# Attention of a transformer layer: values held in TensorE, probabilities streamed, output left turned

## The chip, the cores and the metric

The kernel runs on one core of a Trainium2 chip. The metric is the device time of one execution in microseconds (us). Matrix products run on TensorE (PE in the profile; its weight loads are shown as PEld), elementwise work on VectorE (DVE), ScalarE (ACT) and GpSimd (POOL), and SyncE (SP) issues nearly all weight transfers.

## The reference, cut to what matters

One layer on 256 tokens of width 2048: feed-forward, attention mixer, feed-forward, gated embedding. Everything is float32. The change lies in the mixer:

```
z = rmsnorm(h, g_mix_pre) @ w_qkv + b_qkv          # 2048 x 4352
oa = dilated_attention(qa, ka, va)                  # 16 heads of 64; three patterns, (128,1) (512,4) (2048,16)
ob = sink_swa_gqa(qb, kb, vb, sinks)                # 16 query heads, 2 key/value heads, window 127, sinks
o = concat(rmsnorm(oa, g_out_a), rmsnorm(ob, g_out_b)) @ w_o + b_o
h = h + rmsnorm(o, g_mix_post)
```

With 256 tokens the three dilated patterns share keys: a key that n patterns see counts n times in numerator and divisor, so head a computes softmax(score + log n) over the 256 keys. Queries of the first 128 tokens see 128 keys, those of the second 128 see all 256: three blocks of 128 x 128 for each head. The sinks add one exponential to each divisor of ob.

## The kernel before, in words

TensorE does one long stream of slots. A slot is a chunk of 256 rows x 512 columns of a weight matrix: SP loads it to `raw` (ring of 4), ACT rounds it to `w_high` (L888), DVE subtracts to get `w_rest` (L1201), and TensorE makes 12 matmuls of 512 columns (3 products x 2 row chunks x 2 token tiles; `products`, L470 to L472). A slot's buffer is free once TensorE has used the slot (`w_used`), and `w_rest_done` lets TensorE in. So ACT and DVE work up to four slots ahead.

In the mixer the slots are counted by L: 68 slots of w_qkv (nine blocks of columns, the order is QKV_BLOCKS), then 32 of w_o. Each engine runs its own loop over L, written out in Python, and the small work of attention is hung on fixed values of L, after the slot's matmuls on TensorE. This fixes the order on every engine; only semaphores tie the engines together.

Heads go in 16 pairs of two, the eight pairs of ob first. For each pair, every four slots:

- `turn_pair` (L703): transposes of q (and k), 2 or 4 of 128 x 128, into `pair_bank`; ACT copies (`pair_out`), DVE takes the rest (`pair_rest`, L1470).
- `scores` (L730): 18 products, the two heads on the two halves of the array's rows (64 rows each), L748.
- DVE `soften` (L1440): adds distance times slope to the scores (L1445), two maxima, negated peak. ACT `exps` (L1058): exponentials into `prob`.
- `turn_prob` (L755): three transposes of 128 x 128 for each head, L758. ACT (ob) copies them to `prob_T` or DVE (oa) multiplies them by the turned counts (`prob_T_out`, L1475).
- `weigh` (L762): for each head three float32 products, with a block of `prob_T` stationary (128 x 128) and the values moving (66 columns: 64 and two of ones, whose sum is the divisor), L771 to L773, to `o_bank`.
- DVE `pair_o` (L1482): reciprocal of the divisor, times `o_bank`, into `z`.

The counts are turned once (`turn_count`, three transposes). Then `turn_o` (L780) transposes o back in eight units of four transposes (L569 with `z`), ACT and DVE make `x_high` and `x_rest` from them, and the slots of w_o use these. ACT squares o for the two norms (`square_o`), POOL makes the factors (`factor`, L426). Before the change POOL does nothing else in the mixer than such factors on single columns.

Of the kernel before, what the change touches and what calls it, by code (L numbers as in the profile page):

```python
# [9 lines left out]

# [13 lines left out]
P = 128  # L24
NB = 512
# [9 lines left out]
VW = HD + 2  # L35


def layer_program(nc, x, p, g_ffn1_pre, w_ffn1_gate, w_ffn1_up, w_ffn1_down, g_ffn1_post,
# [60 lines left out]
    U_O = U_MIX + XU  # L99
    U_X2 = U_O + XU  # L100
# [11 lines left out]
    OBLK = AW // NB  # L112
# [11 lines left out]
    def norm_width(job):  # L124
        return AW if job in (J_OA, J_OB) else D

    squares = [T * (OBLK if j in (J_OA, J_OB) else NBD) for j in range(NJOB)]
# [8 lines left out]
    HALVES = [(0, 0), (1, 0), (0, 1), (1, 1)] + [(nb, half) for nb in range(2, NBD) for half in range(2)]  # L136
    WO_SLOTS = ([(hb, k) for hb in (0, 1) for k in range(HU)] + [(hb, k) for hb in (2, 3) for k in range(HU, XU - 1)]
                + [(hb, XU - 1) for hb in (2, 3)]
                + [(hb, HU * HALVES[hb][1] + k) for hb in range(4, 2 * NBD) for k in range(HU)])
# [12 lines left out]
    L_HEAD = L_KEYS + 1  # L152
    L_PAIR = [L_KEYS - 1] + [L_HEAD + 4 * pr - 2 for pr in range(1, PAIRS - 2)] + [L_HEAD + 4 * PAIRS - 11, L_HEAD + 4 * PAIRS - 5]
    L_COUNT = L_PAIR[5] + 2

    G_VALS = BH + AH // 2
    WEIGH_AT = [L_HEAD + 2 * h + 2 for h in range(G_VALS)] + [NSLOT + d for d in (0, 1, 3, 3, 5, 6, 8, 10)]
    PAIR_O_AT = [L_HEAD + 4 * q + 5 for q in range(G_VALS // 2)] + [NSLOT + d for d in (2, 4, 7, 11)]

    O_TURN_AT = [NSLOT - KS + 1 + k for k in range(HU)] + [NSLOT + d for d in (2, 4, 7, 12)]  # L160
    assert len(WEIGH_AT) == H and len(PAIR_O_AT) == PAIRS and len(O_TURN_AT) == XU
# [18 lines left out]
    with ExitStack() as ctx:  # L180
# [48 lines left out]
        vals = sb("vals", [P, T, AH + KVH, VW])  # L229
        bias_row = sb("bias_row", [P, QKV])  # L230
        k_swap = sb("k_swap", [P, T, KVH * HD])
        kb_high = sb("kb_high", [P, 2, S], F32R)
        kb_rest = sb("kb_rest", [P, 2, S], F32R)
        qk_high = sb("qk_high", [P, 2, 2, S], F32R)
        qk_rest = sb("qk_rest", [P, 2, 2, S], F32R)
        dist_i = sb("dist_i", [P, 3 * P], I32)
# [5 lines left out]
        count_T = sb("count_T", [P, 3 * P])  # L242
# [3 lines left out]
        prob_T = sb("prob_T", [P, PTR, 3 * P])  # L246
        peak = sb("peak", [P, 2, T])
# [63 lines left out]
        def wait_prob_T(eng, h):  # L311

            if h < BH:
                eng.wait_ge(prob_T_b, h + 1)
            else:
                eng.wait_ge(prob_T_a, h - BH + 1)
# [1345 lines left out]
```

## Time and profile before

| | |
|---|---|
| median of 3 runs (range) | 1927.27 us (1927.13 to 1927.98) |
| the profiled execution | 1927.2 us |
| its span | 1925.3 us |
| busy: PE, PEld, DVE, ACT, POOL | 1911.9, 1586.7, 1046.8, 875.5, 45.2 us |
| granted TensorE clock | 0.999 |

The span is the time between the first and the last instruction of the profile; the execution has 1.9 us more around it. Busy is the sum of an engine's instruction times. Matmuls overlap, so a matmul's own duration (390 ns for 512 columns) is not what it costs: that is the distance from its start to the start of the next.

### The profile page before, as it was taken

What the parts mean: (1) busy time and instruction counts of PE and PEld (TensorE: products, weight loads), DVE (VectorE), ACT (ScalarE), POOL (GpSimd) and SP (SyncE); (2) the same over time, 40 slices, a digit from 0 to 9 for tenths busy, and PEclk for the clock granted to TensorE, in tenths of its full rate; (3) what the DMA queues carried; (4) which work ended last, traced back from release to release, by engine and by line L of the source; (5) the groups of instructions that cost most, each with busy time, mean ns of one, the idle gap of its engine ahead of it and who ended that gap; (6) DMA issues with size and microseconds to landing.
All of it is one profiled execution on the core that took longest, in us unless ns stands there. A gap on an engine that the chain in (4) does not pass through costs nothing.

```text
span 1925.3 us, 24947 instructions
## 1 busy us (share of the span) xinstructions
PE 1911.9 (99%) x8929; PEld 1586.7 (82%) x8929; DVE 1046.8 (54%) x1199; ACT 875.5 (45%) x1125; POOL 45.2 (2%) x102
## 2 busy tenths in 40 slices
PE   9999999999999999999999999999999999999998
PEld 8888888888888888888888788888888888888886
DVE  5445445444544447676776754454554554444575
ACT  6444444444344346445455644444444444344563
POOL 1000000000000001000000100000000000000010
PEclk9999999999999999999999999999999999999999
DMA  7666666666565655655455466666666666656554
GB/s 249 189 187 192 187 189 186 190 187 191 194 200 194 202 196 163 194 153 165 151 176 181 149 206 191 191 188 193 187 189 191 185 192 201 202 192 203 193 189 142
DMA packets 188484, 361.06 MB, mean 188 GB/s; under 512 B 11440, under 2 KB 16000, under 8 KB 188032
## 3 DMA queue, kind: packets, MB, share of 16 engines
q1 hardware_dynamic: 187408, 356.69, 61.0%
q10 hardware_dynamic: 1008, 3.46, 0.5%
q8 instruction: 43, 0.70, 0.1%
q14 instruction: 25, 0.20, 0.0%
HBM read 358.01 MB, written 2.10 MB: 187 GB/s over the span
## 4 chain that ended last, share of the span: by engine, by line
PE 98%; DVE 1%; ACT 0%; issue 0%; POOL 0%; DVEq 0%; POOLq 0%; ACTq 0%
PE bank L470 31%; PE bank L472 31%; PE bank L471 31%; PE bank L569 2%; PE bank L748 1%; PE bank L758 1%; DVE w_rest L1201 0%; PE bank L772 0%; PE bank L773 0%; PE bank L610 0%; PE bank L771 0%; DVE resid L1225 0%; PE bank L716 0%; DVE x_rest L1216 0%; ACT w_high L888 0%
## 5 line engine op out<-in xcount | busy, mean ns | idle before, releaser
L1201 DVE TENSOR_TENSOR w_rest<-raw,w_high 128x1024 fp32r<-128x1024 f32 x656 | 802.0, 1224 | 757.8 <-ACT w_high L888 757.0
L888 ACT CAST w_high<-raw 128x1024 fp32r<-128x1024 f32 x656 | 686.9, 1049 | 901.9 <-PE bank L472 900.3
L470 PE MATMUL bank<-w_high,x_high 128*128 128x512 f32 (+1 forms) x1920 | 754.3, 393 | 0.5 <-issue 0.2
L472 PE MATMUL bank<-w_high,x_rest 128*128 128x512 f32 (+1 forms) x1920 | 745.1, 388 | 0.0
L471 PE MATMUL bank<-w_rest,x_high 128*128 128x512 f32 (+1 forms) x1920 | 743.9, 387 | 0.0
L472 PEld LDWEIGHTS bank<-w_high,x_rest 128*128 128x128 f32 x1920 | 360.5, 188 | 74.9
L470 PEld LDWEIGHTS bank<-w_high,x_high 128*128 128x128 f32 x1920 | 360.7, 188 | 73.8 <-issue 2.6
L471 PEld LDWEIGHTS bank<-w_rest,x_high 128*128 128x128 f32 x1920 | 361.0, 188 | 70.5
L470 PE MATMUL bank<-w_high,h_high 128*128 128x512 f32 x704 | 274.2, 390 | 0.0
L472 PE MATMUL bank<-w_high,h_rest 128*128 128x512 f32 x704 | 273.9, 389 | 0.0
L471 PE MATMUL bank<-w_rest,h_high 128*128 128x512 f32 x704 | 273.9, 389 | 0.0
L471 PEld LDWEIGHTS bank<-w_rest,h_high 128*128 128x128 f32 x704 | 132.2, 188 | 27.5
L470 PEld LDWEIGHTS bank<-w_high,h_high 128*128 128x128 f32 x704 | 132.2, 188 | 27.5
L472 PEld LDWEIGHTS bank<-w_high,h_rest 128*128 128x128 f32 x704 | 132.2, 188 | 27.0
L431 POOL TENSOR_SCALAR msq<-stat 128x1 f32<-128x1 f32 x20 | 6.2, 308 | 1619.8 <-ACT junk L899 1619.2
L962 ACT ACTIVATE branch<-bank,rstd 128x512 f32<-128x512 f32 x44 | 27.9, 686 | 34.7 <-PE bank L472 32.4
L1216 DVE SCALAR_TENSOR_TENSOR x_rest<-bank,gain_T,x_high 128x256 fp32r<-128x256 f32 x68 | 29.7, 478 | 22.7 <-ACT x_high L913 22.5
L913 ACT ACTIVATE x_high<-bank,gain_T 128x256 fp32r<-128x256 f32 x68 | 28.5, 471 | 20.9 <-PE bank L569 18.1
L1312 DVE SCALAR_TENSOR_TENSOR branch<-bank,rstd,branch 128x512 f32<-128x512 f32 x44 | 31.0, 747 | 9.8 <-PE bank L472 9.8
L1062 ACT ACTIVATE prob<-score,neg_peak 128x256 f32<-128x256 f32 x32 | 16.3, 510 | 32.6 <-DVE neg_peak L1457 16.5
L435 POOL TENSOR_TENSOR msq<-msq,stat 128x1 f32<-128x1 f32 x52 | 24.6, 474 | 240.2 <-ACT junk L899 237.3
L1322 DVE TENSOR_TENSOR h_rest<-bank,h_high 128x512 f32 (+1 forms) x44 | 28.2, 683 | 2.3 <-ACT h_high L970 2.3
(147 smaller groups left out, 675.2 us busy)
## 6 DMA issues: line engine op xcount, KB each, us to landing
raw<-in_w_ffn_gate SPq DMA_DIRECT2D x176, 512.0 KB, 4.4
raw<-in_w_ffn_up SPq DMA_DIRECT2D x176, 512.0 KB, 3.7
raw<-in_w_ffn_down SPq DMA_DIRECT2D x176, 512.0 KB, 4.1
raw<-in_w_qkv SPq DMA_DIRECT2D x68, 512.0 KB, 3.8
raw<-in_w_o SPq DMA_DIRECT2D x32, 512.0 KB, 3.7
raw<-in_w_ple_gate SPq DMA_DIRECT2D x32, 512.0 KB, 4.4
resid<-in_x SPq DMA_DIRECT2D x8, 256.0 KB, 6.7
gain_row<-in_g_ffn_post SPq DMA_DIRECT2D x8, 256.0 KB, 3.8
```

The source lines that it names most:

```text
L435: step(nc.gpsimd.tensor_tensor(msq[:, job, t:t + 1], msq[:, job, t:t + 1], part[b], ALU.add))
L470: nc.tensor.matmul(o[:, 0:width], xh, wh, start=first and c == 0, stop=False)
L471: nc.tensor.matmul(o[:, 0:width], xh, wr, start=False, stop=False)
L472: ins = nc.tensor.matmul(o[:, 0:width], xr, wh, start=False, stop=last and c == chunks - 1)
L569: ins = nc.tensor.transpose(b[:, (c * T + t) * P:(c * T + t + 1) * P], src(t, c), ident[:])
L888: nc.scalar.copy(slot(n, k)[0], raw[:, k]).then_inc(w_high_done, 1)
L913: ins = nc.scalar.activation(x_high[:, CPS * k + c, :], b[:, c * S:(c + 1) * S], ACT.Copy, scale=gain_T[:, gain + c:gain + c + 1])
L962: ins = nc.scalar.activation(silu_g[:, t, :], acc[b0 % 2][t][:], ACT.Silu, scale=rstd[:, job, t:t + 1])
L1201: nc.vector.tensor_tensor(to_rest, raw[:, k], to_high.bitcast(F32), ALU.subtract).then_inc(w_rest_done, 1)
L1216: ins = nc.vector.scalar_tensor_tensor(out=x_rest[:, CPS * k + c, :], in0=b[:, c * S:(c + 1) * S], scalar=gain_T[:, gain + c:gain + c + 1] ...
L1312: ins = nc.vector.scalar_tensor_tensor(out=hidden[:, t, :], in0=acc[(b0 + 1) % 2][t][:], scalar=rstd[:, job, t:t + 1], in1=silu_g[:, t, :] ...
L1322: nc.vector.tensor_tensor(h_rest[:, chunks, :], turn[j][:].rearrange("p (c s) -> p c s", c=CPS), h_high[:, chunks, :].bitcast(F32), ALU.su ...
```

## The change

- `weigh` works on a pair: the values of a head (128 x 64) are stationary, `prob_T` moves. The keys of the first tile go over all 256 queries, those of the second over 128 queries ("two pieces"). The output of the even head goes to partitions 0 to 63 of `o_bank`, that of the odd head to 64 to 127, and it is o transposed. Four products a pair in place of six. `turn_prob` puts its blocks in another order for this and does both heads of a pair behind one another.
- There are no columns of ones in `vals`. The exponentials' instructions on ACT give their sums (`accum_out`), DVE adds the sink and takes the reciprocal (`normalise`), and POOL multiplies `prob` by it (`scale_probs`) before `turn_prob`.
- As o comes out turned, `turn_o` is gone. ACT copies `o_bank` to `z` (`o_out`) and makes `x_high` from it (`o_unit`), DVE makes `x_rest` (`o_rest_unit`).
- The log of the counts is added to the scores instead of multiplying the probabilities: `turn_count` and DVE's `prob_T_out` are gone, POOL prepares a table for each head of oa (`table_of`) and `soften` adds it. ACT copies `prob_T` of all 32 heads (`prob_out`).
- The squares for the norms are made by POOL (`square_pair`) and summed over partitions by TensorE (`sum_squares`, two products with two columns, twice), and DVE copies the sums (`sums_out`).
- The heads start four slots later (L_HEAD = 18 for 14) and the last weighing is at slot 14 of w_o. The slots of w_o go through all four column blocks of the first half of rows and then of the second.
- `bias_row` holds 2048 columns as a ring of four blocks; `gain_mix` has a place of its own and is loaded behind the last scores.

```diff
-    HALVES = [(0, 0), (1, 0), (0, 1), (1, 1)] + [(nb, half) for nb in range(2, NBD) for half in range(2)]
+    HALVES = [(nb, half) for half in range(2) for nb in range(NBD)]
+    WO_SLOTS = [(hb, HU * HALVES[hb][1] + k) for hb in range(2 * NBD) for k in range(HU)]
...
-    L_HEAD = L_KEYS + 1
+    L_HEAD = L_KEYS + 5
+    L_SCORE = [L_HEAD + 4 * p for p in range(PAIRS)]
+    L_PAIR = [L_KEYS - 1] + L_SCORE[:-1]
+    L_PROB = [at + 3 for at in L_SCORE]
+    L_WEIGH = [at + 4 for at in L_SCORE]
+    L_SUM = [L_PROB[PAIRS_B + 1], L_WEIGH[-1] + 2]
+    O_AT = [NSLOT - KS + 1 + k for k in range(HU)] + [NSLOT - 2, NSLOT, L_WEIGH[13] + 1, L_WEIGH[15] + 1]
...
+            def scale_probs(g):
+                pool.wait_ge(norm_ready, g + 1)
+                step(nc.gpsimd.tensor_scalar(prob[:, g % 2, 0:S], prob[:, g % 2, 0:S], norm[:, g % 2, 1:2], None,
+                                             ALU.mult))
+                nc.gpsimd.tensor_scalar(prob[:, g % 2, S:S + P], prob[:, g % 2, S:S + P], norm[:, g % 2, 0:1], None,
+                                        ALU.mult).then_inc(prob_ready, 1)
+            def square_pair(q):
+                pool.wait_ge(o_ready, q + 1)
+                half, o = q // PAIRS_B, o_place(q)
+                to = square_tmp[:] if q % PAIRS_B else o_square[:, half, :]
+                ins = nc.gpsimd.tensor_tensor(to.rearrange("p (t n) -> p t n", t=T), o, o, ALU.mult)
+                step(ins)
+                if q % PAIRS_B:
+                    step(nc.gpsimd.tensor_tensor(o_square[:, half, :], o_square[:, half, :], square_tmp[:], ALU.add))
...
+            def table_of(g):
+                if g - 2 >= BH:
+                    pool.wait_ge(scores_read, g - 1)
+                step(nc.gpsimd.tensor_scalar(tab[:, g % 2, :], dist_a[:], -head_slope[g] * HD ** 0.5, None, ALU.mult))
+                nc.gpsimd.tensor_tensor(tab[:, g % 2, :], tab[:, g % 2, :], count[:], ALU.add).then_inc(tab_ready, 1)
+            for pr in range(PAIRS):
+                scale_probs(2 * pr)
+                scale_probs(2 * pr + 1)
+                if pr:
+                    square_pair(pr - 1)
+                if pr == PAIRS_B - 1:
+                    pool.wait_ge(tables_ready, 1)
+                if PAIRS_B - 1 <= pr < PAIRS - 1:
+                    table_of(2 * pr + 2)
+                    table_of(2 * pr + 3)
...
-            def weigh(h):
-                wait_prob_T(pe, h)
...
-                nc.tensor.matmul(o[1], w[:, 0:P], vals[:, 0, v, :], start=True, stop=False)
-                nc.tensor.matmul(o[1], w[:, P:2 * P], vals[:, 1, v, :], start=False, stop=True)
-                nc.tensor.matmul(o[0], w[:, 2 * P:3 * P], vals[:, 0, v, :], start=True, stop=True
-                                 ).then_inc(weighed, 1)
+            def weigh(q):
+                pe.wait_ge(prob_T_ready, 2 * q + 2)
+                pe.wait_ge(z_ready, 2 if q < PAIRS_B else 6 if q < PAIRS_B + PAIRS_B // 2 else 9)
+                if q:
+                    pe.wait_ge(o_ready, q)
+                if q == PAIRS_B + 1:
+                    pe.wait_ge(o_summed, 1)
+                for c, keys, queries in ((0, slice(0, S), slice(0, S)), (1, slice(S, S + P), slice(P, S))):
+                    for h in range(2):
+                        g = 2 * q + h
+                        v = AH + g // (BH // KVH) if g < BH else g - BH
+                        ins = nc.tensor.matmul(o_bank[HD * h:HD * h + HD, queries], vals[:, c, v, :],
+                                               prob_T[:, g % PTR, keys], start=c == 0, stop=c == 1)
+                ins.then_inc(weighed, 1)
+            def sum_squares(half):
+                pe.wait_ge(part_ready, 1)
+                pe.wait_ge(o_squared, half + 1)
+                pe.wait_ge(o_ready, PAIRS_B + 1 if half == 0 else PAIRS)
+                for t in range(T):
+                    ins = nc.tensor.matmul(o_bank[:, 2 * t:2 * t + 2], o_square[:, half, t * P:(t + 1) * P], part[:],
+                                           start=True, stop=True)
+                ins.then_inc(o_sum_found, 1)
...
+            def prob_out(h):
+                act.wait_ge(prob_turned, h + 1)
+                if h >= PTR:
+                    act.wait_ge(weighed, h // 2 - 1)
+                nc.scalar.copy(prob_T[:, h % PTR, :], head_bank[h % 2][:, 0:3 * P]).then_inc(prob_T_ready, 1)
+            def o_out(q):
+                act.wait_ge(weighed, q + 1)
+                nc.scalar.copy(o_place(q), o_bank[:, 0:S].rearrange("p (t n) -> p t n", t=T)).then_inc(o_ready, 1)
```

On TensorE the order at one value of L is: the slot, `scores` of pair q, `weigh` of pair q - 1, `turn_pair` of pair q + 1; `turn_prob` of pair q comes three slots later, `weigh` of it one slot after that. On ACT it is: `prob_out`, `high`, `o_out`, `pair_out`, `exps`, `o_unit`. On DVE: `soften`, `normalise`, tables, `project_out`, `rest`, `pair_rest`, `o_rest_unit`.

## Rows read from the trace of the kernel before

**Rows 1.** The page: busy us (share) xcount by engine; granted clock in 40 slices.
```profile
PE 1911.9 (99%) x8929; PEld 1586.7 (82%) x8929; DVE 1046.8 (54%) x1199; ACT 875.5 (45%) x1125; POOL 45.2 (2%) x102
PEclk9999999999999999999999999999999999999999
```
**Rows 2.** Waits of TensorE, whole span: who for whom, us, times, longest.
```profile
PE bank L470 <- DVE x_rest L1216: 1.5, 2, 0.9
PE bank L610 <- POOL ident L420: 1.5, 1, 1.5
PE bank L569 <- DVE resid L1225: 0.5, 1, 0.5
```
**Rows 3.** Timeline of TensorE: a weighing, scores, next slot (start, us, instruction).
```profile
930.34 0.40 PE L472 MATMUL bank<-w_high,x_rest 128*128 128x512 f32 x1
930.57 0.34 PE L771 MATMUL bank<-vals,prob_T 128*128 128x66 f32 x2
930.97 0.39 PE L773 MATMUL bank<-vals,prob_T 128*128 128x66 f32 x2
931.28 0.38 PE L748 MATMUL bank<-qk_high 64*128 64x256 f32 x2
931.91 0.28 PE L748 MATMUL bank<-qk_high,qk_rest 64*128 64x128 f32 x2
932.12 0.50 PE L470 MATMUL bank<-w_high,x_high 128*128 128x512 f32 x1
932.45 0.40 PE L471 MATMUL bank<-w_rest,x_high 128*128 128x512 f32 x1
932.69 0.39 PE L472 MATMUL bank<-w_high,x_rest 128*128 128x512 f32 x1
```
**Rows 4.** The same view: one weighing alone between slots.
```profile
1013.10 0.40 PE L472 MATMUL bank<-w_high,x_rest 128*128 128x512 f32 x1
1014.24 0.39 PE L471 MATMUL bank<-w_rest,x_high 128*128 128x512 f32 x1
```
**Rows 5.** The same view: four transposes of o between slots.
```profile
1025.74 0.39 PE L472 MATMUL bank<-w_high,x_rest 128*128 128x512 f32 x1
1025.97 0.60 PE L569 MATMUL bank<-ident,z 128*128 128x128 f32 x4
1026.64 0.39 PE L471 MATMUL bank<-w_rest,x_high 128*128 128x512 f32 x1
```
**Rows 6.** TensorE by line: durations ns min/median/max, first and last start, shapes.
```profile
L771 PE MATMUL bank<-vals,prob_T x64: 223/272/275, 795.2 to 1019.9; 128*128 128x66 f32 x64
L758 PE MATMUL bank<-ident,prob x96: 270/272/328, 792.1 to 1017.0; 128*128 128x128 f32 x96
L748 PE MATMUL bank<-qk_high x32: 218/301/382, 902.5 to 1006.6; 64*128 64x256 f32 x16, 64*128 64x128 f32 x16
```
**Rows 7.** POOL's groups by line: busy us, mean ns.
```profile
L435 POOL TENSOR_TENSOR msq<-msq,stat 128x1 f32<-128x1 f32 x52 | 24.6, 474 | 240.2 <-ACT junk L899 237.3
L431 POOL TENSOR_SCALAR msq<-stat 128x1 f32<-128x1 f32 x20 | 6.2, 308 | 1619.8 <-ACT junk L899 1619.2
L451 POOL IOTA dist_i<- 128x256 int32 x1 | 0.3, 341 | 0.0
L452 POOL IOTA dist_i<- 128x128 int32 x1 | 0.2, 235 | 0.0
```
**Rows 8.** DVE's and ACT's groups in the mixer, same columns.
```profile
L1201 DVE TENSOR_TENSOR w_rest<-raw,w_high 128x1024 fp32r<-128x1024 f32 x656 | 802.0, 1224 | 757.8 <-ACT w_high L888 757.0
L1073 ACT COPY prob_T<-bank 128x384 f32<-128x384 f32 x16 | 7.5, 472 | 0.0
L899 ACT ACTIVATION_READ_ACCUMULATOR junk<-z 128x1 f32 x8 | 1.5, 186 | 0.0
```
**Rows 9.** Busy us of PE, PEld, DVE, ACT, POOL in a stretch of one pair.
```profile
945.00:960.00 15.00, 15.00 (x90) 12.77 (x89) 11.62 (x21) 7.00 (x11) 0.00 (x0) 1.00 0.48 143
```

More of the change, by code:

```diff
@@ L124, in norm_width @@
     def norm_width(job):
-        return AW if job in (J_OA, J_OB) else D
-    squares = [T * (OBLK if j in (J_OA, J_OB) else NBD) for j in range(NJOB)]
+        return AW if job in O_JOBS else D
+    squares = [0 if j in O_JOBS else T * NBD for j in range(NJOB)]
     Q = [sum(squares[:j]) for j in range(NJOB + 1)]
@@ L428, in factor @@
                 n, eps = squares[job] // T, share(job) * EPS
-                part = [stat[:, job, t, b:b + 1] for b in range(n)]
-                pool.wait_ge(squared, Q[job] + T * (n - 2) + t + 1)
-                step(nc.gpsimd.tensor_scalar(msq[:, job, t:t + 1], part[0], eps, None, ALU.add))
+                sums = [stat[:, job, t, b:b + 1] for b in range(n or 1)]
+                if job in O_JOBS:
+                    pool.wait_ge(o_summed, O_JOBS.index(job) + 1)
+                else:
+                    pool.wait_ge(squared, Q[job] + T * (n - 2) + t + 1)
+                step(nc.gpsimd.tensor_scalar(msq[:, job, t:t + 1], sums[0], eps, None, ALU.add))
                 for b in range(1, n):
@@ L829, in _ @@
                     turn_shared_keys()
-                for h in range(H):
-                    if L == WEIGH_AT[h]:
-                        weigh(h)
-                    if L == L_HEAD + 2 * h + 1:
-                        turn_prob(h)
-                for pr in range(PAIRS):
-                    if L == L_HEAD + 4 * pr:
-                        scores(pr)
-                    if L == L_PAIR[pr]:
-                        turn_pair(pr)
-                if L == L_COUNT:
-                    turn_count()
-                for k in range(XU):
-                    if L == O_TURN_AT[k]:
-                        turn_o(k)
+                for q in range(PAIRS):
+                    if L == L_SCORE[q]:
+                        scores(q)
+                for q in range(PAIRS):
+                    if L == L_WEIGH[q]:
+                        weigh(q)
+                for q in range(PAIRS):
+                    if L == L_PAIR[q]:
+                        turn_pair(q)
+                    if L == L_PROB[q]:
+                        turn_prob(2 * q)
+                        turn_prob(2 * q + 1)
+                for half in range(2):
+                    if L == L_SUM[half]:
+                        sum_squares(half)
             ffn(S_FFN2, B_FFN2, U_X2, U_H2, 1)
@@ L1438, in table_a, with table_log @@
                 step(nc.vector.tensor_tensor(dist_a[:], dist_a[:], dist[:], ALU.add))
+            def table_log():
+                two, three = (HD ** 0.5 * math.log(n) for n in (2, 3))
+                logs = tab[:, 0, :]
+                step(nc.vector.tensor_scalar(logs, count[:], 2.0, two, ALU.is_equal, ALU.mult))
+                step(nc.vector.tensor_scalar(count[:], count[:], 3.0, three, ALU.is_equal, ALU.mult))
+                nc.vector.tensor_tensor(count[:], count[:], logs, ALU.add).then_inc(tables_ready, 1)
             def soften(g):
```

291 lines of the change are left out of this document (135 added, 156 removed).

## The prediction

> **What bounds the kernel now.** I read the page first, then TensorE's waits, then its timeline in the mixer. The page shows TensorE busy for 1911.9 of 1925.3 us at the full clock in every slice, DVE at 54%, ACT at 45%, POOL at 2% [rows 1]. The waits of TensorE over the whole span add up to under 5 us, and none of the long ones lies in the pairs of heads [rows 2]. So the end is set by the length of TensorE's stream, and an edit is worth what it takes out of or puts into that stream, unless it makes TensorE wait.
>
> Busy times don't give that length, since matmuls overlap. The timeline does: in a slot one 512-column matmul starts 0.23 us after the other (932.45 to 932.69) [rows 3]. So the price of small work between two slots is the distance from the last matmul before it to the second one behind it, less 2 x 0.227. I take the second because the first one behind small work is itself late to be followed (0.31 to 0.33 us for 0.23).
>
> - Weighing one head alone: 1013.10 to 1014.24 is 1.14, less 0.45 makes **0.69 us** [rows 4].
> - Four transposes of o: 1025.74 to 1026.64 is 0.90, less 0.45 makes **0.44**, or 0.11 each [rows 5].
> - A weighing with scores: 930.34 to 932.45 is 2.11, less 0.45 makes 1.66. The weighing begins at 930.57, the last two of its six pieces at 930.97 (the row stands for both, 0.11 apart), and the scores at 931.28; without the scores the next instruction would come 0.22 to 0.23 after 930.97. So the weighing is 0.63 of the 1.66 and scores with their entry and exit are 1.03 [rows 3].
>
> **TensorE, what goes.** 32 weighings: three stand alone at 0.69, the others beside other small work at 0.63, 20.3 us. Eight units of `turn_o` at 0.44: 3.5. `turn_count`, three transposes at 0.11: 0.3. Together **24.1 us**.
>
> **TensorE, what comes: the pair's weighing.** First how float32 streams. Each weighing product appears twice in the trace (64 pieces for 32 heads), so a float32 product is two passes. The first piece of a head, whose weights were loaded beforehand, lasts 223 ns for 66 columns; the shortest score matmul, single-pass with 128 columns, lasts 218 [rows 6]. 66 columns thus last as long as 128 do: a float32 pass spends two steps of the clock on a column. The transposes agree: 128 float32 columns last 270 and come 0.11 apart, where 0.055 would be one step each at 2.4 GHz [rows 5, 6]. So today's pieces of 66 columns need 0.055 us of streaming, but come 0.11 apart, which is what the load of 128 stationary columns allows. The new form loads only 64 columns and streams 256 or 128: a pass of the first piece needs as long as 512 single-pass columns, 0.227, and one of the second 0.11.
>
> A pair has 4 passes of 0.227 and 4 of 0.11, in the order even, even, odd, odd. If the halves of the array work side by side, a pass of the odd head starts with the second pass of the even one, because instructions start in order and each half does one after the other. Starts: 0; 0.23 and 0.23; 0.45 and 0.45; 0.56; 0.68; 0.79. Then the drain. The scores show it: from their last start to the next slot's 0.21 pass, of which 0.055 is streaming, so 0.15 is drain, and the slot's second matmul is another 0.1 late [rows 3]. The weighing stands behind scores, which pay one such exit anyway; the exit moves to the weighing's end, and between the two there is another drain. So w = 0.79 + 0.11 + 0.15 = **1.05 us** a pair.
>
> Bounds for w: nothing at all side by side gives 4 x 0.227 + 4 x 0.11 + 0.15 = 1.50. Below, the halves entirely parallel (each half streams 2 x 0.227 + 2 x 0.11 = 0.67) and no drain between gives 0.67 to 0.8. I take 1.05, because the two score matmuls of a pair start together in one row (x2) although they use different halves, rows there and columns here. 16 x 1.05 = **16.8 us**. The first and the last weighing have no scores beside them: 2 x 0.2 more.
>
> The Trainium skill (TensorEngine Tiling (Array Packing), Key Properties) says that changing the tiling mode drains TensorE. The trace agrees, with the 0.15 us behind the scores. The page would charge the change in mode and not the change of half. If it holds for every change of half too, that is the third rival.
>
> **The rest on TensorE.** `sum_squares`: two times two products of two passes, load-bound at 0.11 each, 0.9 us. The six transposes of a pair behind one another cost 6 x 0.11 = 0.67 in place of 2 x 0.35, 16 x 0.03 = 0.5 less. Scores, `turn_pair` and all slots stay as they are. The new order of w_o's slots changes nothing in their number.
>
> **Does TensorE wait?** A pair lasts four slots and 3.2 us of small work, some 14 us. Count from the start of `scores`. They end at 0.85, then weigh, turn_pair, and the slot L+1 starts at 2.5; slots end at 5.3, 8.0, 10.7, and `turn_prob` follows. On the other side: `soften` of the even head is done at about 2.3 (4 operations, 1.4 us); ACT does `o_out` and `pair_out` first, which wait for TensorE's weigh and turn_pair (2.5), and the exponentials are ready at 4.4, with 2 x 0.19 for reading the sums [rows 8]. The odd head's come behind ACT's `high` of slot L+1, which waits for 5.3: 6.3 + 1.3 = 7.6. `normalise` of it on DVE is at about 7.8, and where a block is projected (every other pair, 2 x 0.75 more ahead of a `rest` of 1.22) at 8.9. Then POOL scales: 256 and 128 columns.
>
> POOL's price is not in the trace of before: it has only one-column operations, at 308 and 474 ns, and two iotas, 341 for 256 and 235 for 128 columns, 0.83 ns a column [rows 7]. From these a scaling is 0.52 + 0.41 = 0.93 us (below: the iotas' 0.34 + 0.24 = 0.58; above: double the slope and a wait of one DVE operation of 1.22, 2.5). So `prob` is ready at 8.7 to 9.8, and at 10.7 + 0.33 TensorE wants the odd head. Cover 1.2 to 2.3 us; with the upper price it is gone in the pairs with a projection, 0.4 to 0.5 us each in seven pairs. I put **0.5 us** in the sum. The load on POOL in a pair of oa is 2 scalings, 2 squares, 2 tables: 1.9 + 1.6 + 3.1 = 6.6 of 14 us, so it keeps up.
>
> From `turn_prob` to `weigh` lies a slot: ACT's two copies of 0.47 [rows 8] end 1.4 us after the transposes start, TensorE comes at 3.4. Behind them on ACT `high` is 1.4 late; the slot is wanted three slots (8.2 us) later, with 1.05 and 1.22 between, so no wait. DVE loses the product with the counts (0.56) and `pair_o` (0.6 + small) and gains little; in a full pair it had 11.6 of 15 us, ACT 7.0 [rows 9]. ACT gains 4 x 0.19, a 0.47 copy in oa and `o_out`, about 1.6: 8.6 of 14. Neither becomes the bound. The last pair is weighed at slot 14 of w_o and its unit used at slot 19; no wait.
>
> **Sum.** Profiled execution 1927.2 (span 1925.3 and 1.9 around; the median of the runs is 1927.3, so no correction). 1927.2 - 24.1 + 16.8 + 0.4 + 0.9 - 0.5 + 0.5 = **1921.2 us**.
>
> **Rivals.**
> 1. *No side by side.* The halves take turns; w = 1.50, 7.2 us more: **1928.4**, no change. For: every other product of the kernel with 128 rows takes the array alone, and only 64-row matmuls show overlap. Against: the pairs x2 of the scores. Chance 0.17.
> 2. *POOL is late* (the place: TensorE at L_PROB waits for `prob_ready`). DVE and POOL may hinder each other, and then the scaling of the odd head takes over 2.5 us. Every us beyond its cover costs 1 us in each of 16 pairs. It decides from 0.38 us a pair (6 us in all, back to before); at 0.8 us a pair the time is 1921.2 + 12.8 = **1934**. Against: cover of 1.2 to 2.3 us. Chance 0.08. The Trainium skill (SBUF — State Buffer, Who interferes with whom) states such a lock: a DVE instruction with two SBUF inputs, as L1201 is, excludes a GpSimd instruction that reads SBUF. Nothing in the trace of before shows it, as POOL reads nothing wide there.
> 3. *Each change of half drains the array.* Three changes of 0.15 to 0.2 in a pair on top of taking turns, w = 2.0: 1921.2 + 15.2 = **1936**. Decides from w = 1.43. For: the entry to and exit from the scores both cost. Chance 0.06.
> 4. *Better than I count*: w of 0.7 to 0.8, because odd and even start together or no drain lies behind the scores: 1921.2 - 5 = **1916 to 1917**. Chance 0.07.
>
> The forecast has the remaining 0.62.
>
> **Range and chances.** A measurement tells from no change what is over 0.2%, 3.9 us: below 1923.4 is faster. The forecast's own range is 1919 to 1924 (w from 0.9 to 1.2). The range of 8 in 10 takes in rival 1 with 1.5 us of waits: 1917 to 1930. Faster: nearly all of the forecast and rival 4, 0.66. Same: rival 1, an upper part of the forecast, some of rival 2: 0.23. Slower: 0.11.
>
> **What would show it.** In the timeline of TensorE behind scores: the starts of the eight passes; even and odd sharing a start, last pass 0.8 us behind the first, and the next slot 0.26 behind that. L569 with `z` gone. In the waits of TensorE: no line for POOL's `prob` above 1 us in total. POOL's rows: TENSOR_SCALAR 128x256 near 0.5 us. I am wrong if the pair's eight passes start one by one over 1.3 us, if TensorE waits for `prob` by more than 3 us in total, or if a slot's matmuls are no longer 0.227 apart.

## Result, and the profile after

The changed kernel takes **1938.35 us** (median of five runs, 1937.9 to 1938.62) against 1927.85 for the kernel before beside it (1927.13 to 1928.21). The ratio is 1.0056, 95% interval 1.0044 to 1.0067: slower by 10.5 us. Forecast were 1921.2 us and a range of 1917 to 1930, so both the direction and the range were wrong. What happened is in the main rival 2, POOL late at `turn_prob`, which had a chance of 0.08 and a price of 1934. The profiled execution took 1938.45 us (span 1936.6).

The page of the changed kernel first, the line that answers to [rows 1] and the chain's shares by engine:

```profile
PE 1905.4 (98%) x8838; PEld 1570.0 (81%) x8838; DVE 1043.9 (54%) x1194; ACT 889.7 (46%) x1205; POOL 180.9 (9%) x226
PE 87%; POOL 5%; DVE 4%; ACT 2%; issue 1%; DVEq 0%; POOLq 0%; ACTq 0%
```

TensorE is busy for 6.5 us less than in [rows 1] and the span is 11.3 us longer. An engine that works less and ends later waits more. The chain of the kernel before had PE at 98% and POOL at 0%; now POOL, which is busy for 9% of the span, holds 5% of the chain. The waits of TensorE, against [rows 2] (line waited for; us in total, times, longest):

```profile
PE bank L790 <- POOL prob L462: 16.5, 17, 2.2
PE bank L548 <- DVE resid L1261: 1.8, 1, 1.8
PE bank L512 <- DVE x_rest L1252: 1.6, 2, 0.9
```

The first line is new: `turn_prob` waits for POOL's second multiplication. The second is the first transpose behind the mixer, where the kernel before waited 0.2 us. The third was there before.

**The sum, with the forecast's own ruler.** I took the price of every group of small work between two slots as the prediction did (distance from the last 512-column matmul before it to the second one behind it, less 2 x 0.227). In the mixer they come to 57.9 us before and 66.8 us after. Of the 66.8, the groups of `turn_prob` take 15 x 1.956 + 1.84 = 31.2 us, where six transposes without a wait are 0.667 each, 10.7 in all. So 20.5 us are waiting and 46.3 us are work. The work fell by **11.6 us** and the waiting rose by **20.5**; with 1.6 more at the boundary behind the mixer the balance is +10.5, the difference of the medians. The match is closer than the method: the two profiled spans differ by 11.3, and a short stretch at half clock (told below) is in the second. The waits are not even: the groups of `turn_prob` go from 0.98 us to 3.54, and 13 of the 20.5 lie in the eight pairs of oa. The 20.5 are more than the 16.5 of the view because a wait also costs the restart: in the pair below, 0.89 of idle time makes its group 1.11 longer (1.777 for 0.667).

**One pair, engine by engine.** `scores` of this pair starts at 900.26. TensorE at the weighing, as in [rows 3] (start, us, instruction):

```profile
899.95 0.39 PE L514 MATMUL bank<-w_high,x_rest 128*128 128x512 f32 x1
900.26 0.39 PE L779 MATMUL bank<-kb_high,qk_high 64*128 64x256 f32 x2
900.89 0.28 PE L779 MATMUL bank<-kb_high,qk_rest 64*128 64x128 f32 x2
901.10 0.87 PE L806 MATMUL bank<-prob_T,vals 128*64 128x256 f32 x8
901.90 0.44 PE L754 MATMUL bank<-ident,z 128*128 128x128 f32 x2
902.31 0.48 PE L512 MATMUL bank<-w_high,x_high 128*128 128x512 f32 x1
902.63 0.39 PE L513 MATMUL bank<-w_rest,x_high 128*128 128x512 f32 x1
```

All eight passes of a pair start within 0.6 us, and the next group comes 0.80 us behind the first of them: better than forecast. POOL in the same pair:

```profile
906.91 1.74 POOL L460 TENSOR_SCALAR prob<-prob,norm 128x256 f32<-128x256 f32 x1 [8.54 <-DVE norm L1531]
908.75 0.61 POOL L462 TENSOR_SCALAR prob<-prob,norm 128x128 f32<-128x128 f32 x1
909.33 1.89 POOL L460 TENSOR_SCALAR prob<-prob,norm 128x256 f32<-128x256 f32 x1
911.31 0.61 POOL L462 TENSOR_SCALAR prob<-prob,norm 128x128 f32<-128x128 f32 x1
```

POOL sat idle for 8.54 us, got the even head's divisors at 906.9, and its four multiplications took until 911.92 without a gap. The odd head's `norm` was ready at 908.14 (DVE, next fence) but stood behind the even head until 909.33. DVE:

```profile
906.66 1.20 DVE L1237 TENSOR_TENSOR w_rest<-raw,w_high 128x1024 fp32r<-128x1024 f32 x1
907.97 0.17 DVE L1531 RECIPROCAL norm<-exp_sum 128x2 f32<-128x2 f32 x1
909.20 1.23 DVE L1237 TENSOR_TENSOR w_rest<-raw,w_high 128x1024 fp32r<-128x1024 f32 x1 [1.07 <-ACT w_high L919]
```

Both long multiplications of POOL, 1.74 and 1.89, lie over a `w_rest` of DVE that began 0.25 and 0.13 us earlier; the narrow ones without such a neighbour take 0.61, and over all pairs the shortest wide one takes 921 ns. It is so in the whole trace. Of the 64 multiplications 23 overlap no DVE instruction with two SBUF inputs, and these take 0.92 to 0.97 us (wide) and 0.60 to 0.61 (narrow). The 27 that take 1.6 us or more all overlap one. TensorE at `turn_prob`:

```profile
910.59 0.49 PE L790 MATMUL bank<-ident,prob 128*128 128x128 f32 x3
911.97 0.55 PE L790 MATMUL bank<-ident,prob 128*128 128x128 f32 x3 [0.89 <-POOL prob L462]
```

It comes 10.33 us behind `scores` (forecast 10.7), finds the even head, and waits for the odd one. POOL's groups over the span, which [rows 7] could not show (busy us, mean ns):

```profile
L460 POOL TENSOR_SCALAR prob<-prob,norm 128x256 f32<-128x256 f32 x32 | 44.0, 1375 | 124.3 <-DVE norm L1531 124.1
L462 POOL TENSOR_SCALAR prob<-prob,norm 128x128 f32<-128x128 f32 x32 | 33.0, 1033 | 3.0
L481 POOL TENSOR_SCALAR tab<-dist_a 128x384 f32<-128x384 f32 x16 | 19.9, 1242 | 0.9
L482 POOL TENSOR_TENSOR tab<-tab,count 128x384 f32<-128x384 f32 x16 | 19.2, 1202 | 1.3
```

A head costs 1.375 + 1.033 = 2.41 us in the mean, where the forecast took 0.93.

**Behind the mixer.** DVE's last work on the first half of the tokens, for which TensorE's first transposes wait, before the change and after it:

```profile
1074.10 0.74 DVE L1521 SCALAR_TENSOR_TENSOR branch<-bank,rstd,branch 128x512 f32<-128x512 f32 x1
1076.68 1.27 DVE L1225 SCALAR_TENSOR_TENSOR resid<-branch,rstd,resid 128x256 f32<-128x256 f32 x3 [1.84 <-POOL rstd L436]
```

```profile
1081.86 1.29 DVE L1582 TENSOR_TENSOR branch<-branch,gain_mix 128x512 f32<-128x512 f32 x2
1083.06 1.22 DVE L1237 TENSOR_TENSOR early_rest<-raw,early_high 128x1024 fp32r<-128x1024 f32 x1
1084.20 0.74 DVE L1573 SCALAR_TENSOR_TENSOR branch<-bank,rstd,branch 128x512 f32<-128x512 f32 x1
1086.78 1.28 DVE L1261 SCALAR_TENSOR_TENSOR resid<-branch,rstd,resid 128x256 f32<-128x256 f32 x3 [1.84 <-POOL rstd L437]
```

`resid` follows 2.6 us behind the evacuation of the bank (the first line before, the third after) in both. But TensorE's last 512-column matmul ahead of the transposes starts at 1076.89 before and at 1085.15 after. The evacuation stands 2.8 us ahead of that before and 0.95 after: it is 1.8 us late. An `early_rest` is directly ahead of it in both (from 1072.96 before); the products with the gain are there only after.

This wait has a tail. In the profiled execution the granted clock falls to 0.5 (1.2 GHz) behind the 1.78 us in which TensorE did nothing, and stays there for 3.4 us from 1088.0: matmuls of 512 columns start 0.42 us apart, where it is 0.227 at 2.4 GHz. Half of 3.4 us, 1.7, is an estimate of what it cost in this execution. Experiment 1 and the second kernel of experiment 3 have the same wait of 1.8 us, and no such fall behind it, so it doesn't come with every such wait.

### The profile page after: what moved, and what is told of

It reads as the page before. It is cut to its first block, busy times and chain, and to the rows that moved or that the text cites. A ratio compares the mean times of both kernels' runs of the same rounds, so it can differ in the third digit from the quotient of the medians.

```text
span 1936.6 us, 24941 instructions
## 1 busy us (share of the span) xinstructions
PE 1905.4 (98%) x8838; PEld 1570.0 (81%) x8838; DVE 1043.9 (54%) x1194; ACT 889.7 (46%) x1205; POOL 180.9 (9%) x226
## 4 chain that ended last, share of the span: by engine, by line
PE 87%; POOL 5%; DVE 4%; ACT 2%; issue 1%; DVEq 0%; POOLq 0%; ACTq 0%
PE bank L512 28%; PE bank L514 28%; PE bank L513 28%; POOL prob L460 2%; POOL prob L462 2%; PE bank L611 2%; DVE peak L1500 1%; DVE score L1496 0%; POOL tab L482 0%; DVE score L1491 0%; POOL tab L481 0%; PE bank L779 0%; DVE neg_peak L1508 0%; ACT prob L1098 0%; DVE w_rest L1237 0%
## 5 line engine op out<-in xcount | busy, mean ns | idle before, releaser
L1237 DVE TENSOR_TENSOR w_rest<-raw,w_high 128x1024 fp32r<-128x1024 f32 x656 | 803.6, 1227 | 792.5 <-ACT w_high L919 791.9
L460 POOL TENSOR_SCALAR prob<-prob,norm 128x256 f32<-128x256 f32 x32 | 44.0, 1375 | 124.3 <-DVE norm L1531 124.1
L1106 ACT COPY prob_T<-bank 128x384 f32<-128x384 f32 x32 | 15.4, 480 | 44.5 <-PE bank L790 44.5
L1252 DVE SCALAR_TENSOR_TENSOR x_rest<-bank,gain_T,x_high 128x256 fp32r<-128x256 f32 x52 | 22.7, 478 | 22.3 <-ACT x_high L944 22.1
L462 POOL TENSOR_SCALAR prob<-prob,norm 128x128 f32<-128x128 f32 x32 | 33.0, 1033 | 3.0
```

Source lines behind the costliest of these rows:

```text
L460: step(nc.gpsimd.tensor_scalar(prob[:, g % 2, 0:S], prob[:, g % 2, 0:S], norm[:, g % 2, 1:2], None, ALU.mult))
L462: nc.gpsimd.tensor_scalar(prob[:, g % 2, S:S + P], prob[:, g % 2, S:S + P], norm[:, g % 2, 0:1], None, ALU.mult).then_inc(prob_ready, 1)
L1237: nc.vector.tensor_tensor(to_rest, raw[:, k], to_high.bitcast(F32), ALU.subtract).then_inc(w_rest_done, 1)
L1252: ins = nc.vector.scalar_tensor_tensor(out=x_rest[:, CPS * k + c, :], in0=b[:, c * S:(c + 1) * S], scalar=gain_T[:, gain + c:gain + c + 1] ...
```

## Experiments

The kernels keep the whole change but for the edit shown, unless another one is named as their base. The letters in the expectations are theories: A, POOL's multiplications themselves make it late; D, its squares and tables do; E and G, the products with the gain or the order of w_o's units make the boundary late. The others are told in the expectation in which they stand; H, I and N are about the waits for `prob` that are left.

**1. DVE multiplies.** On DVE, in `normalise`, with `scale_probs` gone from POOL:

```
 step(nc.vector.reciprocal(norm[...], exp_sum[...]))
+nc.vector.tensor_scalar(prob[:, g % 2, 0:S], ..., norm[:, g % 2, 1:2], None, ALU.mult)
+nc.vector.tensor_scalar(prob[:, g % 2, S:S + P], ..., norm[:, g % 2, 0:1], None, ALU.mult).then_inc(prob_ready, 1)
```

> The changed kernel, but DVE instead of POOL multiplies prob by the reciprocals, right behind them. Theory A (POOL's scaling, gating turn_prob, is what costs): in the trace of the changed kernel the 16 groups of transposes cost 31.2 us where 16 x 0.667 = 10.7 is their work, so 20.5 us are waits; DVE scales in under 0.7 us a head and all but 1 us of it goes: 1938.4 - 20 = 1918 us, TensorE's wait for prob under 1 us in total. Theory B (the exponentials and normalise come late, POOL only adds its length): only POOL's extra length goes, some 0.5 us a pair, 1930 us. Theory C (POOL disturbs DVE by its squares and tables, w_rest comes late): little goes, above 1934.

Measured: 1923.24 us, ratio to before 0.9979 (0.997 to 0.9989). TensorE's waits and DVE's two new groups:

```profile
PE bank L788 <- DVE prob L1531: 4.6, 7, 1.6
PE bank L546 <- DVE resid L1259: 2.0, 2, 1.8
```

```profile
L1530 DVE TENSOR_SCALAR prob<-prob,norm 128x256 f32<-128x256 f32 x32 | 13.2, 412 | 1.1
L1531 DVE TENSOR_SCALAR prob<-prob,norm 128x128 f32<-128x128 f32 x32 | 11.5, 358 | 0.0
```

A head costs DVE 0.77 us where it costs POOL 2.41. The place of two multiplications alone is worth 15.1 us and turns the change from slower to faster. Of the three theories A is the nearest, but the time is 5 us above its 1918: some 6 us of waiting stay, nearly all of it in the pairs of oa (the second half), where POOL still makes tables and squares.

**2. POOL scales, but does little else.** Squares only for the last pair of each half, and only the first two tables of distance and log count, so the norms and the scores of 14 heads are not the layer's.

> The changed kernel with POOL's other work left out: of the squares only the last pair of each half is squared, and only the first two tables are made (the norms and the scores of 14 heads are not those of the reference). POOL still scales. Theory A (each scaling's own length and start set the wait): POOL idles before every first scaling anyway (8.5 us before the one at 906.9), so most of the wait stays; what goes is only what squares and tables held up DVE with in the pairs of oa, 2 to 5 us: 1933 to 1937. Theory D (POOL is simply overloaded by ten operations a pair): nearly all 20 us go, 1918 to 1920.

Measured: 1930.7 us, 1.0017 (1.0008 to 1.0026). TensorE's waits, then POOL's multiplications (busy us, mean ns):

```profile
PE bank L790 <- POOL prob L462: 10.1, 11, 1.7
```

```profile
L460 POOL TENSOR_SCALAR prob<-prob,norm 128x256 f32<-128x256 f32 x32 | 39.6, 1238 | 176.0 <-DVE norm L1531 175.8
L462 POOL TENSOR_SCALAR prob<-prob,norm 128x128 f32<-128x128 f32 x32 | 31.9, 996 | 3.0
```

Squares and tables account for 7.7 us of the time (7.1 by the ruler); 13.4 us of the 20.5 stay (the groups of `turn_prob` mean 1.55 us for 0.667) with a POOL that has little but the multiplications, at 2.23 us a head. So A carries about two thirds and D one third. The time lies in neither of the ranges put down, 2.3 us below A's. Most of what D takes comes by way of DVE: in the three pairs with the longest waits the odd head's divisors are ready 0.7 to 1.0 us sooner behind `scores` than with the tables.

**3. The products with the gain earlier.** `HALF_LAST[hb] + 3` becomes `+ 2`; alone, and with edit 1.

> The changed kernel with DVE's gain multiplication of a finished column block of w_o two slots behind the block's last one, not three. Theory E (the new order of w_o's slots puts the third block's gain, 1.29 us, ahead of the last accumulator's evacuation on DVE, and TensorE waits 1.8 us for resid at the boundary where it waited 0.2): 1.3 to 1.6 us less, 1936.8 to 1937.0, TensorE's wait for resid back under 0.5. Theory F (the boundary is late for another reason): no change, 1938.3.

> DVE scales and the gain is a slot earlier. If the two act in different places they add up: 1938.4 - 20 - 1.5 = 1917 us, 10.9 less than the kernel before (ratio 0.9944). That is the work counted in the traces: small work on TensorE in the mixer 57.9 us before, 46.3 without waits after. If DVE becomes the bound in pairs with a projection (11.6 of 15 us busy before, some 1.3 more now), waits of TensorE for prob or w_rest of 0.3 to 0.5 us a pair stay: 1920 to 1924.

Measured: 1938.54 us, 1.0059 (1.0045 to 1.0073), and 1923.05, 0.9978 (0.9969 to 0.9987). Neither time differs from its base. The trace of the first is less plain: its waits for `prob` are 15.0 us in place of 16.5, and twice, from 974.7 and from 1022.5, the granted clock is 0.5 for 3.4 us. DVE in the second:

```profile
1066.39 1.28 DVE L1583 TENSOR_TENSOR branch<-branch,gain_mix 128x512 f32<-128x512 f32 x2
1067.60 2.35 DVE L1235 TENSOR_TENSOR early_rest<-raw,early_high 128x1024 fp32r<-128x1024 f32 x2
1069.87 0.74 DVE L1574 SCALAR_TENSOR_TENSOR branch<-bank,rstd,branch 128x512 f32<-128x512 f32 x1
```

The product moved, but two `early_rest` come behind it and end as late as before: their `early_high` are casts that ACT does behind its own work at the boundary. Theory E falls as I had put it (the product one slot sooner; no greater distance was run). What is left is the order of the units, by which work of two halves of the branch falls due together.

**4. Another order of w_o's units,** on top of edit 1: three blocks take their first half early, two take their second half before the last unit:

```
-HALVES = [(nb, half) for half in range(2) for nb in range(NBD)]
-WO_SLOTS = [(hb, HU * HALVES[hb][1] + k) for hb in range(2 * NBD) for k in range(HU)]
+HALVES = [(0, 0), (1, 0), (2, 0), (0, 1), (1, 1), (2, 1), (3, 0), (3, 1)]
+WO_SLOTS = ([(hb, k) for hb in range(3) for k in range(HU)] + [(hb, k) for hb in (3, 4) for k in range(HU, XU - 1)]
+            + [(hb, XU - 1) for hb in (3, 4)] + [... for hb in range(5, 2 * NBD) for k in range(HU)])
```

> e1 with another order of w_o's slots: the last two half blocks are both halves of block 3 again, the second half of block 2 comes four slots earlier (three first halves, then second halves of blocks 0 and 1 with unit 7 held back, then 2). Theory G (the boundary waits 1.8 us longer since ACT's two squares and DVE's evacuation and gain of block 2, 1.6 + 2.7 us, now fall between the slots just ahead of it and push the early casts, whose rests stand ahead of the last evacuation on DVE): 1.5 us less than e1, 1921.7, TensorE's wait for resid 0.2 to 0.5. Theory F (the boundary is late for another reason): no change, 1923.2.

Measured: 1920.49 us, 0.9964 (0.995 to 0.9978), 2.7 us less than edit 1 alone.

```profile
PE bank L790 <- DVE prob L1533: 4.3, 6, 1.6
PE bank L548 <- DVE resid L1261: 0.2, 1, 0.2
```

The wait for `resid` is 0.2 again, and the group of transposes at the boundary fell from 2.62 to 0.44 us. G holds, with 2.2 us there. Of the other 0.5 us, 0.3 is in the first line (4.6 before). The time is 1.2 us below G's 1921.7.

**5. Base 4, POOL light:** the edit of experiment 2 on top.

> e6 with POOL's squares and tables left out as in e2 (norms and scores are not those of the reference). In e1 6.2 us of waits for prob are left, all but 0.4 of them in pairs of oa, where POOL makes tables. Theory H (POOL's reads of SBUF hold up DVE's two-input operations, w_rest and x_rest from z, and so DVE's scaling): these waits go, 1916 us. Theory I (DVE is simply full in those pairs, with x_rest units and projections): they stay, 1921 to 1922.

Measured: 1914.95 us, 0.9935 (0.992 to 0.9951). TensorE no longer waits for `prob` (0.2 us in all) and the groups of `turn_prob` mean 0.698. This is the change with no wait for `prob`, and without most of its squares and tables: 12.4 us under before, where the ruler gave 11.6 less work. H holds against I: DVE isn't too full, it was held up by what POOL did beside it.

**6. Base 4, the log counts added by DVE;** no tables on POOL, squares stay:

```
+step(nc.vector.scalar_tensor_tensor(out=score[...], in0=dist_a[:], scalar=-head_slope[g] * HD ** 0.5, in1=head_bank[...], op0=ALU.mult, op1=ALU.add))
+nc.vector.tensor_tensor(score[...], score[...], count[:], ALU.add)
```

> e6 without POOL's tables: for the 16 heads of oa DVE adds the log of the counts with an operation of its own (128x384, 0.56 us by the rows of before); squares stay on POOL. DVE has 1.1 us more in a pair of oa, POOL 4.4 less. Theory H: a table holds DVE up by about as much as it saves, so the time is within 1.5 us of e6, 1920 to 1923. Theory I (DVE full): 2 x 0.56 more wait in each of 8 pairs, 1927 to 1930.

Measured: 1918.98 us, 0.9957 (0.9943 to 0.997); TensorE waits for `prob` four times, 2.9 us. Moving the tables gives 1.5 of the 5.5 us between experiments 4 and 5. That is a balance: what they cost on POOL less what DVE's added operations cost, and this run doesn't part the two. Both ranges put down were missed, H's by 1 us; I's 1927 to 1930 is far off.

**7. Both heads on one half of the columns,** base 4. The odd head's weighing goes to the even head's 64 columns of the array (`at` are other columns of the bank), one head behind the other, so o of the odd heads isn't computed where it is read:

```
-for c, keys, queries in (...):
-    for h in range(2):
-        ins = nc.tensor.matmul(o_bank[HD * h:HD * h + HD, queries], vals[:, c, v, :],
+for h in range(2):
+    for c, keys, queries in (...):
+        ins = nc.tensor.matmul(o_bank[0:HD, at], vals[:, c, v, :],
```

> e6 with both heads' products of the weighing on the same half of the array's columns (output partitions 0 to 63, the odd head in the bank's other columns), one head behind the other; o of the odd heads is not computed where it is read. Theory J (the pair's 0.80 us come from the two halves streaming at the same time): eight passes one by one, 0.266 + 3 x 0.216 + 3 x 0.109 + 0.2 = 1.44 us a pair, 0.64 us more in 16 pairs, 10.2 us, less what TensorE waits for prob anyway: 1928 to 1932. Theory K (they come from the shorter weight loads): no change, 1921.5.

Measured: 1928.64 us, 1.0007 (0.9998 to 1.0016), 8.15 us more than base 4. TensorE at one pair:

```profile
898.98 1.51 PE L807 MATMUL bank<-prob_T,vals 128*64 128x256 f32 x8
900.43 0.44 PE L754 MATMUL bank<-ident,z 128*128 128x128 f32 x2
```

Eight passes take 1.51 us where they took 0.87 in two halves; the group is 0.64 us longer (2.870 for 2.228), and alone it is 1.645 for 1.006. Side by side is real, worth about 10 us over 16 pairs by this row, of which 8.15 show in the time, since TensorE now comes later to `prob` and waits less for it (2.7 us for 4.3). J holds, K doesn't. A pair's weighing is 1.44 us in this form, near the 1.50 of my rival 1.

**8. The lock by itself.** A kernel of its own: POOL multiplies 128 or 256 columns by a column of factors, alone and beside one kind of DVE instruction after another.

> Not the layer: a program that only times POOL's and DVE's operations, alone and beside each other (its output is not the reference's). Order of the parts: POOL alone, multiplication by a column of factors 128x256, the same 128x128, by a constant 128x256, product of two tensors 128x256; DVE alone, difference of two SBUF tensors 128x1024; then POOL's multiplication 128x256 beside DVE's difference of two SBUF tensors, beside a difference with one input in PSUM, beside a maximum; POOL's fill beside the difference of two SBUF tensors; POOL's multiplication beside DVE's multiplication by factors. Theory L (an instruction of POOL that reads SBUF and one of DVE with two SBUF inputs exclude each other): alone 0.93, 0.61 and 1.22 us as in the changed kernel's shortest rows; beside each other 1.8 to 2.2 us each, while PSUM input, maximum and fill change neither. Theory M (POOL is slow by itself, 1.4 us on the mean): 1.4 us alone too, and the same beside anything.

Alone, beside differences of two SBUF tiles, beside differences with a PSUM input, and beside DVE's own multiplications by a column (each fence one stretch; busy us, mean ns):

```profile
L66 POOL TENSOR_SCALAR narrow<-narrow,factor 128x256 f32<-128x256 f32 x6 | 5.5, 923 | 7.4 <-DVE top L89 6.9
L68 POOL TENSOR_SCALAR narrow<-narrow 128x256 f32<-128x256 f32 x6 | 5.1, 847 | 0.6 <-POOL narrow L73 0.2
L70 POOL TENSOR_TENSOR narrow<-narrow,narrow 128x256 f32<-128x256 f32 x6 | 4.3, 722 | 0.5 <-POOL narrow L73 0.2
L66 POOL TENSOR_SCALAR narrow<-narrow,factor 128x128 f32<-128x128 f32 x6 | 3.6, 602 | 0.6 <-POOL narrow L73 0.2
```

```profile
L95 DVE TENSOR_TENSOR res<-in_a,in_b 128x1024 f32<-128x1024 f32 x11 | 14.7, 1338 | 0.4
L66 POOL TENSOR_SCALAR narrow<-narrow,factor 128x256 f32<-128x256 f32 x8 | 11.2, 1398 | 5.8 <-DVE top L102 5.1
```

```profile
L97 DVE TENSOR_TENSOR res<-in_a,bank 128x512 f32<-128x512 f32 x12 | 8.2, 687 | 0.4
L66 POOL TENSOR_SCALAR narrow<-narrow,factor 128x256 f32<-128x256 f32 x8 | 7.4, 922 | 5.1 <-DVE top L102 4.5
```

```profile
L101 DVE TENSOR_SCALAR res<-in_a,factor 128x1024 f32<-128x1024 f32 x16 | 12.8, 800 | 0.6
L66 POOL TENSOR_SCALAR narrow<-narrow,factor 128x256 f32<-128x256 f32 x8 | 12.9, 1608 | 3.9 <-DVE top L102 3.2
```

The whole kernel took 109.12 us (one run). POOL's multiplication is 922 ns alone and 922 beside a DVE instruction that reads one tile of SBUF and one of PSUM; beside one that reads two of SBUF, as `w_rest` does, it is 1398 in the mean, nearly the 1375 of the changed kernel. Beside a maximum over one SBUF tile (1220 ns, as long as the difference) it is 922 too, so it isn't the length of DVE's instruction. POOL's twelve fills of 256 columns take 311 ns each beside the difference of two SBUF tiles, and that difference 1225: an instruction of POOL that reads nothing isn't touched. M is out. L holds in what excludes what, but not in its size: 1.8 to 2.2 us were expected of both, and POOL's 1398 and DVE's 1338 (1227 alone) were measured. The Trainium skill (SBUF — State Buffer, Who interferes with whom) says that the two engines share a pair of ports under a lock, and that DVE's second SBUF input takes it; this run and the pair above agree.

**9. ACT multiplies** in place of DVE, on top of experiment 6, and on top of experiment 4 with POOL's tables kept:

```
+def scale_act(g):
+    act.wait_ge(norm_ready, g + 1)
+    nc.scalar.activation(prob[:, g % 2, 0:S], prob[:, g % 2, 0:S], ACT.Copy, scale=norm[:, g % 2, 1:2])
+    nc.scalar.activation(prob[:, g % 2, S:S + P], prob[:, g % 2, S:S + P], ACT.Copy,
+                         scale=norm[:, g % 2, 0:1]).then_inc(prob_ready, 1)
```

> e8 (order of w_o as in e6, DVE adds the log of the counts) with ACT multiplying prob by the reciprocals, behind the exponentials of the odd head and one slot later for it. ACT reads SBUF through no port that POOL's squares or w_rest hold. ACT had 7 of 15 us busy in a pair. Theory H (what is left of TensorE's wait for prob in e8, 4.8 us, is DVE's scaling held up by POOL and by its own load): it goes to under 1 us, 1914.5 to 1915.5, the floor that e7 showed with squares and tables left out. Theory N (the chain exponentials, reciprocal, ACT again is longer than the three slots, as ACT's cast of slot L+2 comes first and it is done at 9.9 us of 10.7): waits of up to 0.3 us a pair, 1917 to 1920.

> e6 with ACT multiplying prob by the reciprocals as in e9, POOL's tables and squares kept. Theory H: the tables hold up only DVE's w_rest and x_rest, which have slots of slack, so the wait for prob goes nearly as in e9: 1915 to 1916.5. Theory I (DVE's reciprocals themselves come late in pairs of oa, behind held-up operations): 2 to 4 us of waits stay, 1917 to 1919.

Measured: 1918.29 us, 0.9954 (0.994 to 0.9967), and 1918.54, 0.9955 (0.9942 to 0.9969). The first is by its median the fastest version that computes everything, 8.9 us under the kernel before; the second is 0.25 us behind it, less than the runs of either spread, so with ACT multiplying it matters little who makes the tables. The second keeps 3.4 us of waits for `prob`, as its theory I had it (2 to 4), but the first, without POOL's tables, keeps 3.1. TensorE's waits in the first, and DVE ahead of its first and third stall:

```profile
PE bank L787 <- ACT prob L1102: 3.1, 3, 1.7
```

```profile
955.05 0.88 DVE L1546 SCALAR_TENSOR_TENSOR x_rest<-z,gain_T,x_high 128x256 fp32r<-128x256 f32 x2
955.85 0.55 DVE L1502 SCALAR_TENSOR_TENSOR score<-dist_a,bank 128x384 f32<-128x384 f32 x1
1003.72 0.88 DVE L1546 SCALAR_TENSOR_TENSOR x_rest<-z,gain_T,x_high 128x256 fp32r<-128x256 f32 x2
1004.52 0.16 DVE L1539 RECIPROCAL norm<-exp_sum 128x2 f32<-128x2 f32 x1
```

All pairs but the first (0.74) and three of oa take 0.66 us at `turn_prob`, and the three take 2.57, 1.63 and 1.56. `x_rest` units stand on DVE ahead of `soften` of the odd head in the first two of them, and directly ahead of its reciprocal in the first and the third. H's 1914.5 to 1915.5 was missed by this. The time falls into N's range, but not by N's mechanism of a little in every pair. What is left is DVE's queue ahead of the odd head's divisors. That an order of these units without it reaches 1915 was not run.

## Why the prediction was wrong

**The step that failed** is "POOL's price": "From these a scaling is 0.52 + 0.41 = 0.93 us". Three errors lie in it.

- *Alone*, the two multiplications take 0.92 + 0.61 = 1.53 us (921 and 604 ns at the shortest; 923 and 602 in experiment 8). I took the slope of 0.83 ns a column from the iotas of [rows 7], which read nothing. It is (922 - 602) / 128 = 2.5 ns. The row that was nearest in columns was not nearest in kind.
- *Beside DVE* they take 2.41 us. I had this lock as rival 2, and gave it a chance of 0.08 because nothing in the trace of before shows it. Nothing could: POOL read nothing wide there. But the stretch of [rows 9] had four `w_rest` of 1.22 us (from 947.95, 951.65, 954.09 and 957.56), a third of the time, and in DVE's queue such a one stands close to `normalise`: what sets POOL off is followed by what locks it out. That could be read from the order of DVE's work in the kernel.
- *The cover*. "So `prob` is ready at 8.7 to 9.8" counted one head. In the pair shown `normalise` of the even head stands on DVE behind `pair_rest` and `soften` of the odd one, so both heads' divisors come within 1.4 us (906.7 and 908.1) and POOL does both in one go: 5.0 us from 906.9. `prob` was ready 11.7 us behind `scores`; TensorE wanted the odd head at about 10.8. The cover of "1.2 to 2.3 us" was -0.9. Worked out for this pair, not run: with 1.53 us a head POOL ends at 906.9 + 3.06 = 910.0 and TensorE doesn't wait. So the queue alone would have been covered here, and the lock decides. But only five of the 16 pairs are like this one. In the other eleven POOL takes up the odd head within 0.3 us of its divisors, and these themselves are late: 8.3 to 10.8 us behind `scores`, where the forecast had 7.8 or 8.9, while TensorE comes to `turn_prob` at 10.1 to 10.3 in most pairs and not at 10.7. One head at 2.4 us is too much there.

What each of the three is worth can be worked out from the trace, with the divisors and TensorE's arrival left where they are in each pair (an estimate, not run). With 2.41 us a head the model gives 17.0 us of idle time, where 16.5 were measured. With 1.53, no lock, it gives 5.3, in seven pairs. With the forecast's 0.93 it still gives 2.4, all but 0.2 in three pairs of oa. So the lock is some 11 to 12 us of the idle time, POOL's own speed 3 and the late divisors 2.4, where the forecast had 0.5 in all.

The upper bound that I kept, 2.5 us a head, was right in size. It was set against a cover that was too wide, in the pairs with a projection alone, and moved the sum by 0.5 us where 20.5 were paid. POOL's load in a pair of oa was put too low as well, 6.6 us for a measured 10.6 of 15: the tables are 2 x 2.44, not 3.1.

**"The new order of w_o's slots changes nothing in their number"** is true, and the step left out when DVE has to do what: 1.6 us more of waiting behind the mixer (experiment 4: 2.2 us to be had there).

**The weighing** was 0.80 us a pair and not 1.05, in all 13.05 us and not 17.2. I had the odd head start one pass late. In the trace it starts with the even one, and all eight passes lie in 0.87 us, where each half by my own lower bound streams 0.67, plus an exit. Rival 4's mechanism was the true one for this part (chance 0.07), rivals 1 and 3 were wrong; experiment 7 shows the price of rival 1, 0.64 us a pair. The scores' pairs "x2", which I took for the nearest row, start together too but on different rows of the array.

**Right** were the way of reading (the end is the length of TensorE's stream plus its waits), the removals, `sum_squares` (0.9 forecast, 2 x 0.46), the price of the joined transposes (0.67 forecast, 0.66 measured), and that neither ACT nor DVE becomes the bound, DVE's late divisors apart. The 0.5 us that joining them was to save are not there: three transposes alone were 0.337 before, not 0.35, so it is 0.2 at most. The transposes behind the weighing came 0.05 us cheaper a pair, perhaps since the weighing's exit covers part of their entry; no run shows why. The work of the change is 11.6 us less, against a forecast of 24.1 - 17.2 - 0.9 + 0.5 = 6.5; the waiting ate it and 8.9 us more.

Still open: whether the remaining 3 us of waits in experiment 9 can be ordered away. The lock was not taken out of the changed kernel by itself; its share rests on experiment 8, on the 64 multiplications of the trace and on the estimate above.

## What to carry to other kernels

Before work is given to an idle engine, ask what else it shares: POOL at 2% was idle, and its multiplications ran 1.6 times as long as alone because DVE's two-input instructions, a third of the stretch, stand next in line to what POOL waits for. Price an operation that the trace lacks by a row of its kind (what it reads, with what factor). Where only a row of another kind exists, carry the upper bound from the latest input of any pair, through what stands ahead of it in the queue, before calling it covered. Where TensorE's stream is the bound, an idle engine's lateness costs in full once its cover is gone; here DVE, "busier" by far, took the same work in a third of the time and made the change pay.

## What the runs showed of the hardware

- POOL multiplies faster by a second tensor than by a column of factors: 722 ns for 256 columns against 922, and 847 for a constant.
- Beside DVE's multiplication of 1024 columns by a column of factors (one SBUF tile in), POOL's took 1608 ns, more than beside the two-input difference (1398); DVE's took 800 ns in the mean (754 to 846) and were not run alone.
- With both back to back the price of the lock falls mostly on POOL: DVE's difference rose from 1227 to 1338 ns, POOL's multiplication from 922 to 1398.
- Float32 products with 128 rows and 64 stationary columns each run side by side on the two halves of TensorE's columns, both passes of each: 0.87 us for eight passes, against 1.51 on one half.
- Behind 1.78 us without a matmul the granted clock was 0.5 for 3.4 us in the profiled execution of the changed kernel, and 512-column matmuls came 0.42 us apart for 0.227. Behind the same wait in experiment 1 it stayed at 1.
